# A two-block transformer on one Trainium2 core: the streamed operand tiles stand 16, 32, 256 or 512 bytes elsewhere relative to the weights

## The reference, cut to what matters

```python
# block 1, T = 272 tokens
h = h + mixer(rmsnorm(h))                       # layer 0: chunked scan and attention
h = h + squared_relu_mlp(rmsnorm(h))            # 1024 -> 4096 -> 1024
h = h + multiscale_pool(rmsnorm(h))             # layer 1
h = h + squared_relu_mlp(rmsnorm(h))            # from here on only 256 tokens are kept
# block 2, S = 256 tokens; layer 0 mixes by a short convolution, layer 1 by attention
x = x + rms_norm(mix(rms_norm(x)))
x = x + rms_norm((silu(gate) * up) @ w_down)    # conv_ffn: 1024 -> 2*2816, causal conv of width 3, -> 1024
x = x + rms_norm(sigmoid(rms_norm(x) @ w_gate) * (p @ w_proj))
```

## Time and profile before

| | |
|---|---|
| median of 3 runs | 1249.76 us (1247.42 to 1251.17) |
| the profiled execution's own time | 1251.19 us |
| its span, first to last instruction | 1249.4 us |
| PE busy | 1217.3 us, 10110 matmul records |
| DVE busy | 900.1 us |
| ACT busy | 738.9 us |
| granted TensorE clock, mean over the span | 0.992 |

### The profile page before, as it was taken

One profiled execution on the slowest core, in us unless ns is written; L12 is line 12 of the kernel. 1 busy time (PEld: TensorE's weight loads), 2 busy tenths in 40 slices (PEclk: granted clock), 3 DMA queues, 4 the chain that ended last, 5 costly groups with the idle time before them and its releaser, 6 DMA issues.

```text
span 1249.4 us, 24316 instructions
## 1 busy us (share of the span) xinstructions
PE 1217.3 (97%) x10110; PEld 1191.4 (95%) x10110; DVE 900.1 (72%) x1544; ACT 738.9 (59%) x1258; POOL 18.6 (1%) x36
## 2 busy tenths in 40 slices
PE   9999999999999999999999999999999999999997
PEld 9999799999999999999999999999888899999997
DVE  6986566664446776445866999956787778999656
ACT  6873456564445765434555666655767766665655
POOL 1120000000000000000000000000000000000000
PEclk9999999999999999999999999999899999999998
DMA  7233145555552666564763666473374236665640
GB/s 281 85 121 101 35 169 171 184 173 187 167 169 95 217 197 198 191 197 126 232 193 117 199 191 200 148 252 104 121 249 144 85 123 199 193 193 181 222 137 34
DMA packets 59753, 205.51 MB, mean 164 GB/s; under 512 B 6739, under 2 KB 9340, under 8 KB 59516
## 3 DMA queue, kind: packets, MB, share of 16 engines
q1 hardware_dynamic: 57536, 201.21, 50.2%
q10 hardware_dynamic: 2108, 2.75, 0.7%
HBM read 202.87 MB, written 1.06 MB: 163 GB/s over the span
## 4 chain that ended last, share of the span: by engine, by line
PE 73%; DVE 15%; ACT 6%; issue 3%; DMA 2%; ACTq 0%; DVEq 0%; SPq 0%
PE PS L376 57%; PE PS L421 7%; DVE WL L361 4%; PE PS L388 2%; ACT WH L354 2%; DVE GB L1841 2%; DVE YB L1841 2%; DMA RAW<-wpack 1%; DVE FZ L2339 1%; PE PS L470 1%; PE PS L2467 1%; ACT EE L2625 1%; PE PS L528 1%; DVE FL L2327 1%; DVE YB L2321 1%
## 5 line engine op out<-in xcount | busy, mean ns | idle before, releaser
L361 DVE TENSOR_TENSOR WL<-RAW,WH 128x1024 fp32r<-128x1024 f32 (+2 forms) x387 | 461.4, 1197 | 205.9 <-ACT WH L354 205.1
L354 ACT ACTIVATE WH<-RAW 128x1024 fp32r<-128x1024 f32 (+2 forms) x387 | 392.5, 1034 | 206.9 <-PE PS L376 171.8
L376 PE MATMUL PS<-UH,WH 128*128 128x256 f32 (+1 forms) x1464 | 413.2, 282 | 5.9 <-DVE WL L361 3.9
L376 PE MATMUL PS<-UH,WL 128*128 128x256 f32 (+1 forms) x1464 | 409.9, 280 | 0.0
L376 PE MATMUL PS<-UL,WH 128*128 128x256 f32 (+1 forms) x1464 | 409.6, 280 | 0.0
L376 PEld LDWEIGHTS PS<-UH,WH 128*128 128x128 f32 x1464 | 275.9, 188 | 7.3 <-issue 3.6
L376 PEld LDWEIGHTS PS<-UL,WH 128*128 128x128 f32 x1464 | 274.9, 188 | 0.0
L376 PEld LDWEIGHTS PS<-UH,WL 128*128 128x128 f32 x1464 | 274.6, 188 | 0.0
L376 PE MATMUL PS<-HH,WH 128*128 128x272 f32 (+1 forms) x512 | 144.8, 283 | 0.0
L376 PE MATMUL PS<-HH,WL 128*128 128x272 f32 (+1 forms) x512 | 144.7, 283 | 0.0
L376 PE MATMUL PS<-HL,WH 128*128 128x272 f32 (+1 forms) x512 | 144.3, 282 | 0.0
(11 more groups left out here) (414 smaller groups left out, 2075.1 us busy)
## 6 DMA issues: line engine op xcount, KB each, us to landing
RAW<-wpack SPq DMA_DIRECT2D x361, 512.0 KB, 4.2
RAW<-wpack SPq DMA_DIRECT2D x18, 384.0 KB, 3.3
RAW<-wpack SPq DMA_DIRECT2D x6, 256.0 KB, 2.8
C<-cst SPq DMA_DIRECT2D x1, 1072.0 KB, 5.8
HB<-bias_rows ACTq DMA_DIRECT2D x1, 1024.0 KB, 5.3
out<-X SPq DMA_DIRECT2D x4, 256.0 KB, 2.3
X<-xin SPq DMA_DIRECT2D x2, 272.0 KB, 5.3
X<-xin ACTq DMA_DIRECT2D x2, 272.0 KB, 5.5
```

The costliest lines, as they stand in the source:

```text
L354: a.e.activation(WH[n % NH][:, 0:w], RAW[n % NR][:, 0:w], ACT.Copy).then_inc(*a.mark("wh", n))
L361: v.e.tensor_tensor(WL[n % NH][:, 0:w], RAW[n % NR][:, 0:w], WH[n % NH][:, 0:w].bitcast(f32), ALU.subtract).then_inc(*v.mark("wl", n))
L376: ins = t.e.matmul(o, part(n, hw, kw, a, b), x(kx), start=first and not i and not p, stop=last and i == len(kcs) - 1 and p == 2)
```

## The change

Only addresses move. `UHS` begins 4 floats (16 bytes) into `UH` and `ULS` 4 floats into `UL`, where it began 128 floats in (16 bytes further and 512 back, modulo 1024). `HH[1]` and `HL[1]` begin 252 floats in (1008 bytes, which is 16 back modulo 1024). Three unused tiles are put in front of others: 32 bytes ahead of `FH` (this moves `FL`, `GB`, `YB` and `FZ` too), 256 bytes ahead of `OH` and `OL`, 512 bytes ahead of `XH` and `XL` (this moves the scratch tiles behind them). The engines' instructions, their order, their operands' sizes and their waits are the same.

```diff
-        UHS, ULS = packed(UH, 8, 0), packed(UL, 8, 128)
+        UHS, ULS = packed(UH, 8, 4), packed(UL, 8, 4)
...
-        HH[1], HL[1] = packed(HH[1], 32, 0), packed(HL[1], 32, 0)
+        HH[1], HL[1] = packed(HH[1], 32, 252), packed(HL[1], 32, 252)
...
         CY = [sb(f"CY{i}", [128, S], scope=sc) for i in range(4)]
+        sb("PAD1", [128, 64], scope=sc)
         OH_, OL_ = sb("OH", [128, 8, S], f32r, scope=sc), sb("OL", [128, 8, S], f32r, scope=sc)
...
             sc = ExitStack()
+            sb(f"PAD2{layer}", [128, 8], scope=sc)
             FH.append(sb(f"FH{layer}", [128, 22, S], f32r, scope=sc))
...
         V = sb("V", [128, 2, 1024], scope=sc)
+        sb("PAD3", [128, 128], scope=sc)
         XH, XL = sb("XH", [128, 8, S], f32r, scope=sc), sb("XL", [128, 8, S], f32r, scope=sc)
```

## The result

The changed kernel is slower. Its median is 1261.04 us (1258.53 to 1262.91) against 1248.84 us (1247.42 to 1251.17) of the kernel before beside it: a ratio of 1.0102, 95% interval 1.0086 to 1.0118. (Four executions of each.) That is the place and nearly the price of rival (2), not of the forecast. Its profiled execution took 1261.96 us with a span of 1260.1.

A forecast was written before the change was run, and what follows sets the result against it. PE, busy 97% of the span, bounds the kernel through its matmul spacing; 6.4 us from tight and 9.3 from loose matmuls, less 1.6 for a wait and clock fall, made 14.1 off 1249.8: 1236 us, range 1226 to 1261.

The forecast's parts named there:

- rival (2): Second MLP and convolution input, plus short pieces: the shift leaves only the loose spacing, 1260 us; 0.27 together with rival (4).
- What bounds the kernel: Whole kernel: PE is busy 97% of the span, so the change can act only on how fast instructions follow each other.
- three readings for the address: Load beside stream, filler matmuls at 119 ns, 272-column stages 12 to 13 ns over streaming: distance 64 beats 0 by 6 ns.
- The value of 111 ns for the shifted tiles: Moved tiles' matmuls: spacing falls to 111 ns, near the 110.9 of weight loads alone, if shifted reads stop colliding.
- Tight matmuls outside the FFN ups: Matmuls spaced 113.4 ns outside the FFNs' first halves: (1867 + 800) x 2.4 ns = 6.4 us less.
- loose ones: Matmuls spaced about 117.8 ns outside the FFNs' first halves: (961 + 400) x 6.8 ns = 9.3 us less.
- FFN ups bound by DVE at 120.8 us: Both FFNs' first halves: DVE sets the pace at 120.8 us, so faster matmuls gain zero there.
- The second FFN's wait and clock, -1.6: End of the second FFN up: faster PE would wait for `FL` and the clock fall, costing 1.6 us.
- 256 and 512 bytes worth nothing: Moves of `OH`, `OL`, `XH`, `XL` keep the distance modulo 128: 0, at most 1.3 us either way.
- its 1267: rival (2) with every moved tile at 119 ns and FFN ups bound by PE: 1267 us; chance 0.1, outside the range.
- rival (4): DVE slower on tiles 16 or 32 bytes off; 1% in the FFN ups is 2.4 us; 0.27 together with rival (2).
- The rule of the Trainium skill: All matmuls: loading weights takes no read bandwidth from the running matmul, so distance could not matter; time stays 1249.8 us.

The follow-up runs named there:

- v2: Kernel before with the first MLP's hidden tiles reordered in memory, so distances 64 and 0 no longer alternate: ratio 1.0004 (0.9989 to 1.0018).
- a4_64: Kernel before with all streamed tiles, not the weights, 64 bytes further on (256-column tiles at distance 0 modulo 128): ratio 1.0172.
- m1: Kernel before, second MLP down streaming whole tiles, 128 columns twice, 64 bytes repeated or 16 bytes repeated: 113.3, 113.3, 119.8, 111.7 ns; no time read.
- p1_u: Kernel before with only `UHS` and `ULS` moved, both to 4 floats in: ratio 1.0054 (1.0037 to 1.0071), +6.7 us.
- w1_both: Kernel before with `UHS` and `ULS` at distance 80 in both FFN ups only: 1246.04 us against 1248.56, ratio 0.9982.
- w2_second: Kernel before with `UHS` and `ULS` at distance 80 in the second FFN up only: ratio 0.9994 (0.9985 to 1.0002).
- b2: Kernel before once more, unchanged, one execution: first FFN up 117.7 ns, where its first trace had 113.2; no time read.
- s1: Kernel before with `HH[1]` and `HL[1]` in four blocks at distances 64, 80, 96, 112: first blocks 113.3, 119.2, 118.3, 117.3 ns; no time read.

## Why the prediction was wrong, point by point

- **What bounds the kernel, and that only the spacing can move: right.** The counts are equal and DVE and ACT were as busy. That there are two spacings at distance 64, and that the relation to the weights matters, holds in all the runs above. Of the three readings for the address one was no witness: the 272-column stages are 12 to 13 ns over their streaming at one distance as at the other (v2: 125.2 and 125.8), so they don't show what distance 0 costs 256 columns. The filler matmuls did, and a4_64 bears them out with 120.0.
- **The value of 111 ns for the shifted tiles: wrong, and this is the step that failed.** It came from twelve loads with nothing streaming beside them, with the transposes of the earlier trace rows as a neighbour. Those rows show PE without the collision; they don't show that a shift takes the collision away. The moved tiles measured 119.3 (`U`, 80), 119.2 (`HH[1]`, 48) and 118.3 (`FH`, 96). m1 shows what it takes to reach 111.7: a stream that never leaves 16 bytes. The argument "64 is better than 0, so something else may be better than 64" took two points for a slope. The curve has a single sharp point at 64, and the kernel before stood on it.
- **The sum's signs follow.** Tight matmuls outside the FFN ups were to give 6.4 us and lost 11.5 in the three stages; loose ones were to give 9.3 and gave nothing, since the 118 to 119 of the moved tiles is no better than the 117.8 that they had.
- **FFN ups bound by DVE at 120.8 us: right for DVE**, which needed 120.8 in all four windows. That a change there is worth zero was nearly right: the first FFN as a whole went from 188.2 to 189.7, the second from 187.9 to 187.8. The second kept its time only because its stream happened to run at 116.6 ns; in p1_u, w1_both and w2_second the same up at distance 80 took 127.2 us instead of 125.7. And the zero is not exact for tight ups, which gave 1.5 to 2.3 us (table above) where the down behind the wait was tight again.
- **The second FFN's wait and clock, -1.6: did not come up**, since PE got no faster. As rival (2) had it, the first FFN's wait and clock fall went; but b2 shows that they can be missing in the kernel before too.
- **256 and 512 bytes worth nothing: borne out**, 0.9995 (0.9984 to 1.0006). That `OH` turned tight in the changed kernel is a change of choice, not of address.
- **Rival (2) named the direction, the place and the threshold**: "load and stream take turns exactly; a shift by a part of a block would spoil that". Its 1260 took the loose spacing (117.8), its 1267 took 119 ns with loose tiles and both ups paying too; the measured 119.3 in the tight stages alone gives 1261 (1867 x 5.9 = 11.0 us). That its 1260 came so close is in part luck: each tight matmul of the long stages cost 5.9 ns instead of 4.4, and the short pieces, 800 matmuls and 3.5 us in its sum, nearly cancelled. That load and stream take turns is its picture, and no run shows it; the runs show that the tight spacing goes with distance 64. It had 0.27 with rival (4), too little: the trace had shown a good spacing at 64 and no row that was both shifted and faster with the same form.
- **The rule of the Trainium skill** (TensorE: Matmul & The Clock Gate, Step-by-step) that the load of the next weights takes nothing from the running matmul would have kept the time. The runs differ from it: with the same instructions the second MLP's matmuls came every 113.3 ns at distance 64, 120.0 at 0 and 121.6 at 68, and the measurement decides. It is closest to true for the tight spacing, 2.4 ns over the 110.9 of the load alone.

What stays open is what the load and the stream do to each other, why there are two locked spacings at 64, and what picks one behind a break. I have counts for it, no cause.

## What to carry to other kernels

When each matmul brings its own weight load, measure the spacing from start to start for each stage and note where the streamed tile stands from the weights modulo 128; here, with 256 columns and 128 x 128 weights, 64 was the one distance that could give 113.3 ns (and in other stretches gave 117.8), 0 cost 6.7 ns per matmul more, and four bytes off 8.3. With 272 columns 0 and 64 were nearly alike. Don't take a row without the conflict as the price of a new address: one run with several distances in blocks gives the whole curve. A stage whose pace another engine sets is the place to spend a slower spacing, if what follows gains from it.

## What the runs showed of the hardware that was not expected

- The relation between streamed tile and weights is sharp to 4 bytes: 113.3 ns at 64, 121.6 at 68, 118.3 at 56, 120.0 at 0; moving both together by 32 bytes changes nothing that can be told (0.9996, interval 0.9985 to 1.0007).
- At multiples of 64 bytes the stream locks: 340 ns per three matmuls, or 353 to 354, or 360 at distance 0, with hardly another value in hundreds.
- The same program ran the same stage tight in one execution and loose in another (113.2 and 117.7 ns), which is 3.8 us of one FFN up. The wait, the fall of the clock and the loose down behind them took it back: up and down together were 188.2 us in the tight case and 188.0 in the loose one.
- A long unlocked stream was followed by a tight one in 5 of 5 FFN downs, and 144 unlocked matmuls in s1 by a tight block 3 times of 3; three unlocked matmuls did not do it.
- Off the multiples of 64, too, one distance had more than one spacing: 119.1 and 116.6 ns at 80 in the two FFN ups of one execution.
- A stream that repeats 64 bytes was slower (119.8 ns) than one that walks through a whole tile (113.3); one that repeats 16 bytes was the fastest seen (111.7). One run, m1, shows both.
